# A two-layer diffusion transformer on one Trainium2 core: modulation of the first layer by column halves, between row halves of the input projection

## The reference, cut to what matters

```python
sh1, sc1, gt1, sh2, sc2, gt2 = split(silu(cond) @ w_ada[l] + b_ada[l], 6)   # w_ada[l]: 1024 x 6144
h = rmsnorm(x, norm_mix_pre[l]) * (1.0 + sc1) + sh1
qa, ka, ..., vd = split(h @ w_in[l])                                        # w_in[l]: 1024 x 2400
```

## Time and profile before

| | us |
|---|---|
| median of 3 runs | 1610.06 (1610.03 to 1613.97) |
| the profiled execution | 1610.92 |
| its span, first to last instruction | 1608.7 |
| PE busy | 1526.7 (95%) |
| DVE busy | 1166.4 (73%) |
| ACT busy | 973.0 (60%) |

### The profile page before, as it was taken

How to read it: one execution, slowest core, us unless ns; L and a number is a source line. 1 busy time by engine, 2 the same in 40 slices (tenths; PEclk the granted TensorE clock), 3 DMA queues, 4 the chain that set the end, 5 groups by cost and what they waited for, 6 DMA issues and landing times.

```text
span 1608.7 us, 22084 instructions
## 1 busy us (share of the span) xinstructions
PE 1526.7 (95%) x7825; PEld 1237.4 (77%) x7825; DVE 1166.4 (73%) x1000; ACT 973.0 (60%) x950; POOL 117.8 (7%) x167
## 2 busy tenths in 40 slices
PE   5988999999898889999999999999999999999995
PEld 2866699988676668887887887887887887887884
DVE  2557444435557538888888888888888888888885
ACT  3345443424534446777777777777777777777773
POOL 2420140000020110000000000000000000000001
PEclk9999999999999989999999999999999999999998
DMA  9956664567751377999999999999999999999991
GB/s 369 297 181 211 230 181 157 184 212 265 292 190 65 132 254 284 366 369 349 385 374 354 384 370 349 388 369 347 391 370 345 391 369 353 386 368 342 394 386 53
DMA packets 221317, 484.91 MB, mean 301 GB/s; under 512 B 8800, under 2 KB 41872, under 8 KB 221264
## 3 DMA queue, kind: packets, MB, share of 16 engines
q1 hardware_dynamic: 215024, 466.38, 80.4%
q0 software_dynamic: 6240, 17.80, 4.0%
HBM read 475.34 MB, written 8.81 MB: 301 GB/s over the span
## 4 chain that ended last, share of the span: by engine, by line
PE 88%; DVE 4%; ACT 3%; issue 2%; DMA 1%; POOL 1%; POOLq 0%; SPq 0%; DVEq 0%; ACTq 0%
PE ps L1679 23%; PE ps L1680 23%; PE ps L1684 23%; PE ps L1694 3%; PE ps L1701 3%; PE ps L1695 3%; PE ps L1724 2%; PE ps L2121 2%; PE ps L1902 1%; DMA raw<-in_w_ada 1%; PE ps L1763 1%; ACT w_hi L771 1%; ACT probs L851 1%; DVE sm L1271 1%; DVE qz L1235 1%
## 5 line engine op out<-in xcount | busy, mean ns | idle before, releaser
L1141 DVE TENSOR_TENSOR w_lo<-raw,w_hi 128x2048 fp32r<-128x2048 f32 (+1 forms) x397 | 905.7, 2285 | 211.9 <-ACT w_hi L771 210.7
L771 ACT ACTIVATE w_hi<-raw 128x2048 fp32r<-128x2048 f32 (+1 forms) x397 | 757.9, 1913 | 263.9 <-PE ps L1680 240.3
L1679 PE MATMUL ps<-w_hi,x_hi 128*128 128x512 f32 (+1 forms) x1216 | 435.9, 369 | 4.1 <-ACT w_hi L771 2.7
L1680 PE MATMUL ps<-w_hi,x_lo 128*128 128x512 f32 (+1 forms) x1216 | 430.8, 365 | 0.0
L1684 PE MATMUL ps<-w_lo,x_hi 128*128 128x512 f32 (+1 forms) x1216 | 285.8, 365 | 0.0
L1679 PEld LDWEIGHTS ps<-w_hi,x_hi 128*128 128x128 f32 x1216 | 229.0, 188 | 44.6 <-issue 5.2
L1680 PEld LDWEIGHTS ps<-w_hi,x_lo 128*128 128x128 f32 x1216 | 229.1, 188 | 38.0
L1684 PEld LDWEIGHTS ps<-w_lo,x_hi 128*128 128x128 f32 x1216 | 207.8, 188 | 39.9
L1679 PE MATMUL ps<-w_hi,h_hi 128*128 128x512 f32 x528 | 209.2, 396 | 6.4 <-DVE h_lo L1473 4.3
L1680 PE MATMUL ps<-w_hi,h_lo 128*128 128x512 f32 x528 | 209.3, 396 | 0.0
L1684 PE MATMUL ps<-w_lo,h_hi 128*128 128x512 f32 x528 | 141.7, 393 | 0.0
(11 more groups left out here) (259 smaller groups left out, 1068.8 us busy)
## 6 DMA issues: line engine op xcount, KB each, us to landing
raw<-in_moe_w_gate SPq DMA_DIRECT2D x112, 1024.0 KB, 5.6
raw<-in_moe_w_up SPq DMA_DIRECT2D x112, 1024.0 KB, 6.4
raw<-in_moe_w_down SPq DMA_DIRECT2D x112, 1024.0 KB, 6.4
raw<-in_w_ada SPq DMA_DIRECT2D x48, 1024.0 KB, 5.7
raw<-in_w_in SPq DMA_DIRECT2D x20, 960.0 KB, 11.5
raw<-in_ffn_w_gate SPq DMA_DIRECT2D x11, 1024.0 KB, 5.8
raw<-in_ffn_w_up SPq DMA_DIRECT2D x11, 1024.0 KB, 6.0
raw<-in_ffn_w_down SPq DMA_DIRECT2D x11, 1024.0 KB, 5.0
```

Of the source, the lines that this page charges most:

```text
L771: act.activation(split_hi(c, slice(0, width(c))), raw[:, r % NRAW, 0:width(c)], ACT.Copy).then_inc(hi_done, 1)
L1141: dve.tensor_sub(split_lo(c, n), raw[:, raw_of(c) % NRAW, n], split_hi(c, n)).then_inc(lo_done, 1)
L1679: pe.matmul(out, xh, split_hi(c, w), start=start, stop=False, skip_group_check=True)
L1680: last = pe.matmul(out, xl, split_hi(c, w), start=False, stop=False, skip_group_check=True)
```

## The change

Before, four ada units give the whole scale and four more the whole shift. After, units 4, 5, 0, 1 give scale and shift of features 0 to 511 (still called section (0, 1)) and units 6, 7, 2, 3 those of features 512 to 1023 (section (0, 0)). The stream becomes: ada 4, 5, 0, 1; win 0; ada 6, 7; win 2; ada 2, 3; win 4; win 1, 3, 5; win 6 to 9. An even win unit is the upper row half (features 0 to 511) of a column block.

PE's new list: ada 4, 5, gains, ada 0, 1, transposes, `columns(0, 1)`; then the upper row halves of blocks 0, 1, 2 for both streams, with ada 6, 7 after block 0, ada 2, 3 after block 1's first stream and `columns(0, 0)` after its second; then the lower row halves of blocks 0, 1, 2; then blocks 3 and 4 as before. Three pairs of PSUM banks are open at once, so `proj_copies` goes by j % 3, in layer 1 too. DVE makes h of features 0 to 511 from PSUM by its `norm_h` (L1195) and splits win 0 between the two streams; ACT keeps the transposed features 512 to 1023 in SBUF (`keep_T`) and applies scale and shift to them later. `section(0, *)` now has three small operations. Only 144 of 976 columns of `cst` are loaded at the start; the other 832 and the loads of layer 0 are started by POOL after the third `hi` instead of the second. The copy of the cached rotary key moves from j = 2 to j = 3 on DVE.

The diff, cut to its core:

```diff
@@ -47,10 +47,9 @@
-C_ID, C_UP, C_ONE, C_IOTA, C_ANTI, C_MASK = 0, 128, 256, 384, 512, 640
-C_COS64, C_SIN64, C_COS32, C_SIN32, C_REV8, C_NEGH, C_SEL = 768, 832, 896, 928, 960, 968, 970
-C_TOK, C_DUM = C_SEL + 4, C_SEL + 6
-C_N = C_SEL + 7
+C_ID, C_REV8, C_NEGH, C_SEL, C_TOK, C_DUM, C_FIRST = 0, 128, 136, 137, 141, 143, 144
+C_UP, C_ONE, C_IOTA, C_ANTI, C_MASK = 144, 272, 400, 528, 656
+C_COS64, C_SIN64, C_COS32, C_SIN32, C_N = 784, 848, 912, 944, 976
...
@@ -121,7 +120,7 @@
-            units += ada(0, 4, 5, 6, 7, 0, 1, 2, 3) + win + ada(0, 8, 9, 10, 11)
+            units += ada(0, 4, 5, 0, 1) + win[0:1] + ada(0, 6, 7) + win[2:3] + ada(0, 2, 3) + win[4:5] + win[1:6:2] + win[6:] + ada(0, 8, 9, 10, 11)
...
@@ -143,13 +142,25 @@
-ROW_BANK = {(0, 1): 7, (0, 0): 6, (1, 1): 1, (1, 0): 1}
-COL_BANK = {(0, 1): 7, (0, 0): 6, (0, 4): 6, (1, 4): 6, (1, 5): 7}
+ROW_BANK = {(0, 1): 0, (0, 0): 0, (1, 1): 1, (1, 0): 1}
+COL_BANK = {(0, 1): 1, (0, 0): 1, (0, 4): 6, (1, 4): 6, (1, 5): 7}
...
+def section_of(l, n):
...
+    if l == 0 and n < 8:
+        return (0, 1 - n // 2 % 2), 1 - n // 4, n in (4, 6), n in (1, 3)
+    return (l, n // 4), n // 2 % 2, n % 4 == 0, n % 4 == 3
...
+def section_end(l, k):
...
+    return ada_end(0, 3 - 2 * k) if l == 0 and k < 2 else ada_end(l, 4 * k + 3)
...
@@ -189,6 +200,15 @@
+def win_c(l, j, h):
+    return SPLIT.index(("win", l, 2 * j + h))
...
+def half_count(q, h):
...
+    return 2 * h + q + 1 if q < 2 else 2 * q + h + 1
...
@@ -424,7 +445,7 @@
-            return 4 * s if l or which else 2 * s
+            return 4 * s if l or which else 4 + 2 * s
...
@@ -433,7 +454,7 @@
-            src = ps[:, 2 + 2 * (j % 2) + s, :]
+            src = ps[:, 2 + 2 * (j % 3) + s, :]
...
@@ -605,7 +626,7 @@
             pool.dma_start(rows_c[8:16, :], c_lat[0].rearrange("(k n) -> k n", k=KT)).then_inc(in_c, 16)
-            pool.dma_start(cst[:, :], consts).then_inc(in_cst, 16)
+            pool.dma_start(cst[:, 0:C_FIRST], consts[:, 0:C_FIRST]).then_inc(in_cst, 16)
...
@@ -644,7 +665,8 @@
                 else:
-                    pool.wait_ge(hi_done, 2)
+                    pool.wait_ge(hi_done, 3)
+                    pool.dma_start(cst[:, C_FIRST:C_N], consts[:, C_FIRST:C_N]).then_inc(in_tables, 16)
...
@@ -791,7 +813,7 @@
                     act.wait_ge(col_T, m - 1)
-                act.wait_ge(ada_used, ada_end(l, 4 * k + 3))
+                act.wait_ge(ada_used, section_end(l, k))
...
@@ -820,13 +842,18 @@
-                        src, scale = h[:, P * k:P * k + P], 1.0
+                        src = h[:, P * k:P * k + P]
...
-            def norm_hi(l, which, s):
+            def keep_T(s):
...
+                act.wait_ge(nT, 2 * s + 2)
+                act.activation(h_of(0, 0)[s][:, 512:1024], ps[:, T_bank(0, 0, s) + 1, :], ACT.Copy).then_inc(nkeep, 1)
...
+            def norm_hi(l, which, s, halves=(0, 1)):
...
-                for h in range(2):
+                for h in halves:
...
@@ -1022,11 +1049,17 @@
                     rows(0, 1)
+                    split_to(1)
+                    for s in range(2):
+                        keep_T(s)
+                        norm_hi(0, 0, s, (0,))
+                    split_to(2)
                     rows(0, 0)
+                    split_to(4)
+                    act.wait_ge(nkeep, 2)
...
                         norm_h(0, 0, s)
-                        norm_hi(0, 0, s)
-                        split_to(s + 1)
+                        norm_hi(0, 0, s, (1,))
...
@@ -1048,7 +1081,7 @@
                 for j in range(NWIN):
-                    split_to(min(win_u(l, j) + 3, win_u(l, NWIN)))
+                    split_to(min(win_u(l, j) + 3, win_u(l, NWIN)) if l else (6, 7, 8, 9, 10)[j])
...
@@ -1059,7 +1092,7 @@
                                        proj[0][:, KPE:KPE + 32].unsqueeze(1).to_broadcast([P, 4, 32]), ACT.Copy).then_inc(kp4_ready[0], 1)
-                    split_to(min(win_u(l, j) + 4, win_u(l, NWIN)))
+                    split_to(min(win_u(l, j) + 4, win_u(l, NWIN)) if l else (6, 7, 8, 10, 10)[j])
...
@@ -1177,7 +1210,13 @@
-                if k % 3 == 0:
+                if l == 0 and k < 2:
+                    n = slice(4 - 4 * k, 8 - 4 * k)
+                    dve.tensor_tensor(mod[:, 0, 0, n, :], src[:, 1], b2(bcol[:, 0, 0, n], 2), ALU.add)
+                    link(dve.tensor_tensor(mtmp[:, n, :], src[:, 0], b2(bcol[:, 0, 1, n], 2), ALU.add))
+                    dve.scalar_tensor_tensor(out=mod[:, 0, 1, n, :], in0=mtmp[:, n, :], scalar=1.0, in1=b2(gcol[:, 0, 0, n], 2),
+                                             op0=ALU.add, op1=ALU.mult).then_inc(mod_ready, 1)
+                elif k % 3 == 0:
...
@@ -1197,11 +1236,11 @@
-            def norm_lo(l, which, s):
+            def norm_lo(l, which, s, halves=(0, 1)):
...
-                for h in range(2):
+                for h in halves:
...
-                    dve.wait_ge(nhi, 2 * q + h + 1)
+                    dve.wait_ge(nhi, half_count(q, h))
...
@@ -1545,19 +1584,15 @@
-                    h = [h_of(0, 0)[s].rearrange("p (k t) -> p k t", k=KT) for s in range(2)]
...
-                        dve.wait_ge(nT, 2 * s + 2)
-                        last = dve.tensor_tensor(h[s], ps[:, 2 * s:2 * s + 2, :].rearrange("p a (b t) -> p (a b) t", t=P),
-                                                 b2(mod[:, 0, 1, :, s], P), ALU.mult)
-                    link(last)
+                        norm_h(0, 0, s)
+                        norm_lo(0, 0, s, (0,))
+                        split_to(s + 1)
+                    split_to(3)
...
+                    split_to(4)
...
-                        dve.tensor_tensor(h[s][:, 0:4, :], h[s][:, 0:4, :], b2(mod[:, 0, 0, 0:4, s], P), ALU.add).then_inc(nh[0], 1)
-                    norm_lo(0, 0, 0)
-                    split_to(1)
-                    norm_lo(0, 0, 1)
-                    split_to(2)
+                        norm_lo(0, 0, s, (1,))
...
@@ -1568,23 +1603,24 @@
                 for j in range(NWIN):
-                    split_to(min(win_u(l, j) + 4, win_u(l, NWIN)))
-                    dve.wait_ge(used, win_u(l, j) + 2)
+                    split_to(min(win_u(l, j) + 4, win_u(l, NWIN)) if l else (6, 7, 8, 10, 10)[j])
+                    dve.wait_ge(used, win_c(l, j, 1) + 1)
...
                     if j == 1:
+                        dve.wait_ge(in_tables, 16)
...
                         link(rope(proj[1][:, QB:QB + 512], 16, 32))
+                    if j == 3:
+                        dve.wait_ge(win_evac[1], NWIN * l + 4)
+                        link(rope(proj[1][:, KPE:KPE + 32], 1, 32))
...
                                         kcache[:, K_KPE:K_KPE + 32].unsqueeze(1).to_broadcast([P, 4, 32])).then_inc(kp4_ready[1], 1)
-                    if j == 3:
-                        dve.wait_ge(win_evac[1], NWIN * l + 4)
-                        link(rope(proj[1][:, KPE:KPE + 32], 1, 32))
...
@@ -1712,8 +1748,9 @@
-                r, h, m = AT["ada", l, n], n % 2, SECTIONS.index((l, n // 4))
-                if n % 4 == 0:
+                at, i, first, last_of = section_of(l, n)
+                r, h, m = AT["ada", l, n], n % 2, SECTIONS.index(at)
+                if first:
...
@@ -1721,8 +1758,8 @@
-                    last = pe.matmul(row_ps(m)[CG * kt:CG * kt + CG, :], cond[:, 4 * h + kt, n // 2 % 2, :],
-                                     raw[:, r % NRAW, 512 * kt:512 * kt + 512], start=n % 4 == 0, stop=n % 4 == 3)
+                    last = pe.matmul(row_ps(m)[CG * kt:CG * kt + CG, :], cond[:, 4 * h + kt, i, :],
+                                     raw[:, r % NRAW, 512 * kt:512 * kt + 512], start=first, stop=last_of)
...
@@ -1905,6 +1942,8 @@
+                pe.wait_ge(win_evac[1], NWIN * l + 3)
...
@@ -2193,37 +2232,51 @@
                     pe.wait_ge(cond_ready, 1)
-                    for n in (4, 5, 6, 7):
-                        ada(0, n)
+                    ada(0, 4)
+                    ada(0, 5)
                     pe.wait_ge(in_g, 80)
-                    pe.transpose(ps[:, 4, 0:64], rows_g, ident(64))
-                    pe.transpose(ps[:, 4, 128:224], rows_b, ident(96)).then_inc(init_T, 1)
+                    pe.transpose(ps[:, 2, 0:64], rows_g, ident(64))
+                    pe.transpose(ps[:, 2, 128:224], rows_b, ident(96)).then_inc(init_T, 1)
                     ada(0, 0)
+                    ada(0, 1)
...
                         norm_T(0, 0, s)
-                    ada(0, 1)
                     columns(0, 1)
-                    ada(0, 2)
-                    ada(0, 3)
-                    columns(0, 0)
...
                     norm_T(1, 0, 0)
-                for j in range(NWIN):
+                def w_in_unit(j, h, s):
+                    if j >= 3 and h == 0:
+                        pe.wait_ge(win_evac[s], NWIN * l + j - 2)
+                    if l and j == 2 and h == s == 0:
+                        pe.wait_ge(row_evac, SECTIONS.index((1, 2)) + 1)
+                    if j == 0:
```

(33 more changed lines are left out.)

7 lines of the change are left out of this document (4 added, 3 removed).

## The result

The kernel after took 1594.99 us in the median of 5 runs (1594.59 to 1600.45), the kernel before 1613.60 (1610.03 to 1614.28); the ratio is 0.9901, interval 0.9878 to 0.9923. The forecast was wrong. The profiled execution of after took 1594.59 us with a span of 1592.4, 16.3 less than before.

A forecast was written before the change was run, and what follows sets the result against it. PE was taken to bound the kernel (busy 95%), with time to win only at the start. First product at 27.0, second stream at 31.8, attention at 87.1, 4.6 us earlier: 1610.06 less 4.6 gives 1605.5, range 1603.8 to 1608.4.

The forecast's parts named there:

- What bounds the start: Start of the kernel: PE waits for constants and ada loads, first product at 36.59; from there to 91.71 no idle time.
- The constant load: First load shrinks from 977 columns to 144, so each later load lands 1.11 us earlier (0.98 by the skill's price).
- First product: Start of the projection: the path runs over four loads, not eight, so it starts at 27.0, 9.6 us earlier.
- Second stream: Projection start: after DVE splits win 0 (29.1), the second stream is ready at 31.8; PE should never wait again.
- The rest: Projection from 31.8: 19 calls 49.8 us, four ada units 4.2, columns 1.1, and 0.2 for the clock.
- Attention: End of the projection: the attention's first ada unit starts at 87.1, 4.6 us earlier; wrong if outside 85.5 to 90.
- What must stay hidden: Projection: ACT and DVE work for the second half finishes before PE needs it, with a margin of 0.8 us.
- Rival A: First lower half: the second half's chain is late, PE waits about 2 us, total 1607.5; chance 0.17.
- Rival C: Weight ring: ada 6 keeps its slot until 35.5, win 1 starts late, PE starves, up to 1613.6; chance 0.05.
- Rival B: First calls: the clock falls in PE's 3.5 us gap and returns late, costing 2.6 us, total 1608.1; chance 0.13.
- The step that failed: From the attention on: only the order of waits changes, so the stretch keeps its 1517 us within 1 us.

The follow-up runs named there:

- after_loads_early: Kernel after, with the tables and layer 0 loads started after the first w_hi instead of the third: 1604.26 us, ratio 0.9938 to before.
- after_again: Kernel after, unchanged, measured a second time in another group of runs: 1599.20 us, ratio 0.9914 to before.
- before_976: Kernel before with unused column 969 of cst dropped, giving every tensor its address in after, old schedule: 1602.88 us, ratio 0.9952 to before.
- before_lo0: before_976 with the pads of after_lo0, so its places under the old schedule: 1599.98 us, ratio 0.9925 to before.
- after_lo0: Kernel after with 16 unused columns between x_hi and x_lo and 16 in front of cond: 1592.53 us, ratio 0.9879 to before.
- after_lo0_h64: after_lo0 with 16 more unused columns between h_hi and h_lo: 1593.45 us, ratio 0.9882 to before.
- after_977: Kernel after with cst allocated at 977 columns instead of 976, putting tensors behind it at their old places: 1607.98 us, ratio 0.9967 to before.

## Why the prediction was wrong, point by point

- **What bounds the start** was right: PE waited only for the new, shorter path, once for 3.4 us before the first product and once for 0.6 before the second stream, and never again in the projection.
- **The constant load.** Forecast 1.11 us, measured 0.84 at the fourth load in after, 0.89 alone, and 0.91 between the averages of the four old and the eleven new traces. The estimate of 0.98 from the price by bytes in the Trainium skill ("DMA: Bandwidth & Descriptors", section "Anatomy of one DMA") was the nearer one.
- **First product** at 26.1 where 27.0 was forecast: 0.3 us were lost on the load, and transposes (2.44 for 2.83 + 0.4), columns and section were 1.2 us shorter. Over the eleven traces it stands at 26.0 to 27.4, and the spread goes with the clock: where the clock was at half through most of the transposes, from the first to the last of them took 3.0 to 3.3 us instead of 2.2 to 2.7.
- **Second stream** 30.88 for 31.8. **The rest**: 54.7 us from there to the attention for 55.3 in the sum. **Attention** at 85.57 for 87.1, and 86.4 on average; one of the eleven, at 85.30, is even outside the 85.5 to 90 that I had allowed.
- **What must stay hidden** stayed hidden. Rival A, the chain of the second half, did not occur: no wait at about 45 to 50 us. Rival C, the starving ring, did not occur in after. In after_loads_early a late weight did stop PE, but by POOL's loads in flight beside it and not by a slot, so C's own mechanism stays untested.
- **Rival B, the clock.** After the idle time from 22.7 to 26.1 the clock did fall, but only from 27.3 to 30.7 (0.63 over 26.1 to 30.5, 1.00 over 30.5 to 85.6), within the call that waits anyway: nothing lost in this profile. In the trace of after_again the clock was at half from 24.8 to 31.6, so through the whole first call; the second stream began at 31.39, without a wait for `x_lo` and 0.5 us later than in after, 0.4 of it from the later first product. So B occurred in its mild form. The Trainium skill ("TensorE: Matmul & The Clock Gate", section "Part 1: The HAM clock gate") says that the number of slow matmuls at a kernel's start differs from run to run. The two traces of after agree: half clock from 27.3 to 30.7 us in one and from 24.8 to 31.6 in the other.
- **The step that failed** is the sentence "Nothing behind 91.71 is touched by the change except in its order of waits", which put the change behind the attention at nothing, and with it the test that the stretch behind keeps its 1517 us. It lasted 1506.8. I had followed order, waits, banks and queues into the later layers, and not addresses. before_976 shows that the new addresses alone give 7.7 us (2.4 in the dense layer, 3.7 in the experts, the rest in the other stages and in the clock). Of the 10.2 us won behind the attention, another 3.7 are the routing's, 3.4 of them its clock, which met 17.1 us of half clock in before and 10.2 in after. The addresses didn't do that, since before_976 has 17.1 too. Neither schedule fixes it: the old one met 17.1 in three of its four traces and 10.2 in before_lo0, the new one 10.2 in ten of its thirteen and 17.1 in after_lo0, after_lo0_h64 and after_loads_early. Whether the new schedule makes 10.2 likelier or it was luck is not shown.

The schedule's own effect, 4.7 us at the attention, was forecast at 4.6; in part that is luck, for the new traces reach the attention 0.7 us earlier on average than forecast, and the old ones 0.6 earlier than the 91.71 that I worked from. The whole was 14 to 16, because a second effect of about 8 us came with it (7.7 in before_976, 8.8 between after_977 and after_again). The 1 to 3 us that are left lie within the intervals and the spread of the clock.

## What to carry to other kernels

When a diff changes the size of a tensor in SBUF, work out which tensors behind it move and by how much before calling the rest untouched; in a kernel bound by matmuls that stream from SBUF a shift of 32 bytes under the operands was worth about 8 us, a careful new schedule 4.7. To measure a schedule, hold the addresses still (an unused column or a pad), and try a few placements of the hi and lo operands on their own, each by its stage and not by the sum, as one stage's gain can be another's loss. Note how far every tensor behind a pad has moved, in full bytes: a remainder by 128 hid a move that was worth 4 us. Small loads behind the large ones must be placed by what they delay: 2.2 MB started 20 us too early took back all that the new order had won up to the attention.

## What the runs showed of the hardware that I had not expected

- The rate of back-to-back matmuls, nearly all with 512 moving columns, depends on the addresses of their SBUF operands: 4068 to 4111 of them begin in the same 920 us at full clock, over ten placements, with the same DMA share (1.01 to 1.02), while ACT's and DVE's splits take 1.92 and 2.29 us in all 17 traces. Two kernels with the same addresses and different schedules agree: 926.9 and 927.2, 923.2 in five traces, 919.3 and 919.4, 917.4 twice.
- 256-column products of the dense layer prefer other places (162.4 to 163.5 us with x_hi and x_lo at 64, 165.1 to 166.3 with both at 96 or at 0, 164.4 to 165.4 with the two 64 bytes apart, net of half clock) than the 512-column ones of the experts. Which reader collides with which (PE's two operands, ACT and DVE writing the splits, the DMAs filling `raw`) was not tried.
- The clock's half-speed stretches in the routing of layer 1 hold for 10.2 or 17.1 us, never between, in the 17 traces of nearly equal programs, and the stage is about 3 us longer with the latter. Of one program, after_again's six runs spread over 6 us, with mean granted clocks of 0.975 to 0.980.
